# A chunked two-way RWKV-7 recurrence: the loop over chunks written out on four engines, and two small tiles read in place

## The chip, the cores and the metric

The kernel runs on 1 core of one Trainium2 chip. The metric is the device time of one execution in microseconds (us), smaller is better. The program computes a whole network of two blocks. The change touches one stage of it, the recurrence of the second block's RWKV mixer; all other stages are the same in both kernels.

## What is computed in the stage

The reference, cut to the recurrence (all float32). `x` has 512 latent tokens, the context has 256; there are 16 heads of 64. The recurrence runs forward and backward, first over the context and then, from the context's final states, over the latents.

```python
def _rwkv_step(S, inp):
    r, w, kk, kka, kt, v = inp
    sk = jnp.einsum('bhij,bhj->bhi', S, kk)
    S = S * w[:, :, None, :] - sk[..., None] * kka[:, :, None, :] + v[..., None] * kt[:, :, None, :]
    return S, jnp.einsum('bhij,bhj->bhi', S, r)

# in stream(h, S0): low-rank inputs of the decay and of the rate, one pair for each direction z
dec = w0[:, None, None, :] + jnp.einsum('zbtr,zrd->zbtd', jnp.tanh(jnp.einsum('btd,zdr->zbtr', xw, w1)), w2)
logw = -jax.nn.softplus(-dec) - 0.5
w = heads(jnp.exp(-jnp.exp(logw)))
a = heads(jax.nn.sigmoid(a0[:, None, None, :] + jnp.einsum(
    'zbtr,zrd->zbtd', jnp.einsum('btd,zdr->zbtr', xa, a1), a2)))
...
S_f, y_f = _rwkv_scan(S0[0], (r, w[0], kk, kk * a[0], kt[0], v), False)
S_b, y_b = _rwkv_scan(S0[1], (r, w[1], kk, kk * a[1], kt[1], v), True)
```

## The kernel before, in words

The four compute engines run programs of their own and meet at semaphores. `rwkv_scan` takes the tokens in chunks of 64 (`CH`), in two phases: the context (4 chunks, `lat` false) and the latents (8 chunks, `lat` true). Both directions z = 0 and z = 1 are walked alternately, so that one direction's work fills the other's waits. A call of `both(z, it, y, tail_it, front_it)` is one **step**, and it weaves three things together on every engine:

- the **chain** of direction z, chunk `it`: Gram matrices (`gram`), five levels of squaring of a 64x64 matrix per head (`level`), with the results copied out of PSUM by ScalarE and VectorE and the unit matrix added by GpSimd (`factor`);
- the **tail** of direction y, chunk `tail_it`: `start`, six products `apply` with a copy by ScalarE (`x_out`) between each two, `results`, and `state`, whose product VectorE adds to the state (L2644);
- the **front** of direction y, chunk `front_it`: `decay_rank` and `rate_rank` (TensorE, from the low-rank inputs, called latents), then gates, `cumulate`, keys, `alpha`, `beta`, `kappa`, `rho`, and `end` on GpSimd.

`in_turn` sets the order: two steps ahead of the loop, then a hardware loop (`eng.Fori`, L2188) over `steps - 1` iterations of two steps each, then two steps behind it. Each engine runs this loop itself, with its own counter and its own backward branch. In it a wait compares a semaphore with a value in a register, which register instructions work out from the counter, since the value grows with the iteration (`Events.value`). The loop has 3 iterations in the context phase and 7 in the latent phase, so TensorE's branch goes back 2 + 6 = 8 times.

On TensorE each wait goes through `wait` (L2318), which is an instruction of its own and also adds 1 to a semaphore `begun`, which nobody reads.

The low-rank inputs of all tokens stand in `tw` and `ta`, in the buffer X. GpSimd's `latents` (L2211) copies this step's 64 columns of each into the small tiles `twc` and `tac`; TensorE reads them in `decay_rank` (L2339) and `rate_rank` (L2347). `latents` comes first in a step on GpSimd, thus behind `decayed` and `end` of the step before. TensorE waits for "tokens" before `decay_rank`, and `gram` stands behind `decay_rank` in its queue.

In the program a float32 matmul stands once; in the trace it is two MATMUL with two LDWEIGHTS.

## Time and profile before

| | |
|---|---|
| time, median of 3 runs | 4123.04 us (4122.61 to 4123.76) |
| time of the profiled execution | 4099.76 us |
| its span | 4098.0 us |
| granted TensorE clock, mean of the span | 0.91 |
| the recurrence, from the first step with a chain to the last product | 2579 to 3375 us of the span |

The profile is of one execution, which took 23 us less than the median of the others. The recurrence holds about a fifth of the span. In the rows, PE is a matmul, PEld the load of its weights, PEldq, ACTq, DVEq and POOLq are the engines' sequencers (branches, register instructions and waits), and "idle before <-X" tells what ended the engine's idle time. "issue" is time in which the engine waited for nothing that the profile shows.

### The profile page before, as it was taken

The numbers are of one execution on the slowest core, as the hardware profiler recorded it, in microseconds if no ns is written. First come the engines' busy times: TensorE is split into PE (matmuls) and PEld (weight loads), VectorE is DVE, ScalarE is ACT, GpSimd is POOL, SyncE is SP. The second block draws the span as 40 slices with busy tenths as digits, with TensorE's granted clock in tenths as the row PEclk, the third lists the DMA queues.
The fourth block names the chain that finished last, engine by engine and source line by source line (L and its number), as shares of the span: only waits on it lengthen the run. The fifth ranks groups of instructions, "written<-read, shape, count | busy, mean of one in ns | idle before, by whom it ended". The sixth has DMA issues, their size and how long they took to land. (4 is left out here: it accounts for less than half of the span.)

```text
span 4098.0 us, 85586 instructions
## 1 busy us (share of the span) xinstructions
PE 3343.7 (82%) x37286; PEld 1973.3 (48%) x37286; DVE 1463.6 (36%) x3061; ACT 811.7 (20%) x1666; POOL 462.1 (11%) x448
## 2 busy tenths in 40 slices
PE   6998999896999986999995898776777765678877
PEld 5846476463445643343342444666666662322222
DVE  3656256552025623212213412443444434311111
ACT  2015111241015610000001001443333320100000
POOL 0000000000001100000000000443433320000000
PEclk9998899988999987999997998897989877799999
DMA  5652247302111124999996110000000002299998
GB/s 163 164 186 74 50 118 190 117 22 83 57 48 33 60 82 176 365 346 336 363 345 228 49 48 21 4 4 3 4 4 4 4 13 100 100 399 404 404 402 347
DMA packets 148963, 606.63 MB, mean 148 GB/s; under 512 B 19200, under 2 KB 21824, under 8 KB 131584
## 3 DMA queue, kind: packets, MB, share of 16 engines
q1 hardware_dynamic: 142272, 579.57, 39.0%
q0 software_dynamic: 6336, 21.63, 2.3%
q8 instruction: 308, 5.05, 0.5%
q14 instruction: 47, 0.39, 0.0%
HBM read 576.39 MB, written 31.07 MB: 148 GB/s over the span
## 5 line engine op out<-in xcount | busy, mean ns | idle before, releaser
L1704 PE MATMUL psum<-ring,big 128*64 128x512 f32 (+1 forms) x6144 | 904.8, 500 | 110.2 <-DMA ring<-moe_w 93.6
L1704 PEld LDWEIGHTS psum<-ring,big 128*64 128x64 f32 (+1 forms) x6144 | 301.4, 125 | 674.4 <-issue 472.6
L2297 PE MATMUL psum<-ring 64*64 64x64 f32 x11520 | 250.4, 232 | 100.8 <-issue 75.5
L371 PE MATMUL psum<-h_uT,ring 128*128 128x264 f32 x1280 | 290.5, 387 | 0.0
L2297 PEld LDWEIGHTS psum<-ring 64*64 64x64 f32 x11520 | 218.6, 143 | 129.2 <-issue 117.9
L371 PEld LDWEIGHTS psum<-h_uT,ring 128*128 128x128 f32 x1280 | 242.0, 190 | 46.5 <-issue 5.8
L500 DVE SCALAR_TENSOR_TENSOR h_O<-h_O,cond_silu 128x512 f32<-128x512 f32 x336 | 227.1, 743 | 102.2 <-DMA h_O<-ada_w 102.2
L1215 PE MATMUL psum<-ring,big 128*128 128x512 f32 x576 | 251.1, 596 | 2.0 <-PEq L55 2.0
L1985 PE MATMUL psum<-big,ring 128*128 128x512 f32 (+1 forms) x464 | 171.4, 532 | 31.7 <-DVE big L1956 24.0
L1850 DVE TENSOR_TENSOR big<-big,psum 128x512 f32<-128x512 f32 (+1 forms) x48 | 27.3, 596 | 463.7 <-PE psum L1704 463.7
L2234 POOL TENSOR_TENSOR ring<-ring,eye_sb 128x512 f32<-128x512 f32 x120 | 154.0, 1283 | 222.8 <-PE psum L2297 221.5
L1215 PEld LDWEIGHTS psum<-ring,big 128*128 128x128 f32 x576 | 109.0, 191 | 134.8 <-issue 134.8
L391 PE MATMUL psum<-ring,h_uT 128*128 128x512 f32 x384 | 168.3, 595 | 0.0
L2517 ACT ACTIVATE ring<-psum 128x512 f32<-128x512 f32 x168 | 100.4, 598 | 336.3 <-PE psum L2297 333.1
L1858 DVE SCALAR_TENSOR_TENSOR big<-psum,big,gates 64x512 f32<-64x512 f32 (+1 forms) x128 | 78.8, 615 | 242.8 <-PE psum L1704 241.4
L1001 PE MATMUL psum<-ring,big 128*128 128x512 f32 x320 | 141.3, 605 | 11.0 <-DMA ring<-rw_w_o 9.4
L1985 PEld LDWEIGHTS psum<-big,ring 128*128 128x128 f32 x464 | 90.0, 195 | 112.9 <-issue 108.8
L1784 ACT ACTIVATE big<-psum 128x512 f32<-128x512 f32 (+1 forms) x48 | 23.5, 524 | 566.8 <-PE psum L1704 566.7
L2651 DVE COPY ring<-psum 128x512 f32<-128x512 f32 x96 | 66.4, 691 | 173.7 <-PE psum L2297 173.7
L391 PEld LDWEIGHTS psum<-ring,h_uT 128*128 128x128 f32 x384 | 72.0, 190 | 90.2 <-issue 90.1
L119 PE MATMUL psum<-ident_sb,big 128*128 128x128 f32 x176 | 29.0, 343 | 97.0 <-DVE big L197 97.0
L1001 PEld LDWEIGHTS psum<-ring,big 128*128 128x128 f32 x320 | 61.9, 194 | 89.1 <-issue 79.6
(344 smaller groups left out, 4544.7 us busy)
## 6 DMA issues: line engine op xcount, KB each, us to landing
ring<-moe_w SPq DMA_DIRECT2D x192, 2048.0 KB, 10.8
h_O<-ada_w SPq DMA_DIRECT2D x192, 256.0 KB, 3.0
ring<-w_in SPq DMA_DIRECT2D x16, 2048.0 KB, 14.8
ring<-na_w_qkv SPq DMA_DIRECT2D x6, 2048.0 KB, 8.0
ring<-w_out SPq DMA_DIRECT2D x4, 2048.0 KB, 8.8
bias_rows<-na_table SPq DMA_DIRECT2D x16, 480.0 KB, 15.7
ring<-bias_rows SPq DMA_DIRECT2D x16, 360.0 KB, 2.9
rows<-big SPq DMA_DIRECT2D x10, 512.0 KB, 5.1
```

Source lines behind the costliest of these rows:

```text
L371: last = nc.tensor.matmul(bank(k, pair_bank(q) + h, NH), w[:, a, f * P:(f + 1) * P], uT[:, a, halves[h]], start=a == 0, stop=a == KD - 1)
L391: last = nc.tensor.matmul(bank(k, b), uT[:, a, t * P:(t + 1) * P], w[:, a, :], **st)
L500: nc.vector.scalar_tensor_tensor(into, ada(u), by, into, ALU.mult, ALU.add).then_inc(s.acc, 1)
L1001: last = nc.tensor.matmul(bank(k, j % BANKS)[0:rows, :], srcT[:, a, t * P:t * P + rows], w[:, a, :], start=a == 0, stop=a == KD - 1)
L1215: last = nc.tensor.matmul(bank(k, j % FIRST_BANKS), hT[:, a, t * P:(t + 1) * P], w[:, a, :], start=a == 0, stop=a == KD - 1)
L1704: last = nc.tensor.matmul(bank(k, b, r.width)[q * r.n:(q + 1) * r.n, :], rowsT[:, half * HALF_K + n, r.first:r.first + r.n], w[:, n, q * r ...
L1858: last = nc.vector.scalar_tensor_tensor(y[r.first:r.first + r.n, x % 2, cols], bank(k, r.downs, r.width)[mine, :], gate[mine, x, 2 * r.at ...
L1985: last = nc.tensor.matmul(bank(k, j % BANKS, n), w[:, a, at:at + P], xs[m][:, a, first:first + n], **st)
L2234: ev["pool"][z].done(nc.gpsimd.tensor_tensor(pairs(factors[n], z), pairs(factors[n], z), eye3, ALU.add), f"factor{n}")
L2297: last = nc.tensor.matmul(bank(k, b, CH, at + p % QUAD * CH)[to:to + CH, :], pairs(lhs, z)[lo:lo + CH, p, :], rhs(lo, p), start=start and ...
L2517: ev["act"][z].done(nc.scalar.activation(flat2(T_n, z), side(W(z), 0), ACT.Copy), f"x{n}")
L2651: ev["dve"][z].done(nc.vector.tensor_copy(both_of(n, z, 1), bank(k, U(z) + 1).rearrange("p (e x) -> p e x", e=2)), f"level{n}")
```

## The change

- `in_turn` runs a Python loop instead of `eng.Fori`. The steps of all iterations stand one behind another in the program, on TensorE, ScalarE, VectorE and GpSimd, in the same order as they were run. The values that waits compare with, and the columns that are read, are constants.
- GpSimd's `latents` is gone, with the tiles `twc` and `tac` and the events "tokens" and "rates". `decay_rank` and `rate_rank` read 64 columns of `tw` and `ta` directly, and do not wait for GpSimd.
- TensorE's `wait` no longer adds to `begun`. Where a wait stands just ahead of a matmul the builder now puts it on the matmul itself.

```diff
@@ -2122,7 +2122,7 @@
-        pool=["tokens", "rates", "akk"] + only("bon", "bonus_in") + ["end"])
+        pool=["akk"] + only("bon", "bonus_in") + ["end"])
@@ -2185,7 +2185,7 @@
             both(0, 0, 1, None, 0)
-            with eng.Fori(0, steps - 1) as it:
+            for it in range(steps - 1):
                 both(1, it, 0, it, it + 1)
                 both(0, it + 1, 1, it, it + 1)
@@ -2208,20 +2208,6 @@
-                def latents(z, it, tail_it):
-
-
-                    mine, lo = fr["pool"][z], z * CH
-                    if tail_it is not None:
-                        made("pe", z, tail_it, "iclr")
-                    elif lat:
-                        pool.wait_ge(fr["pe"][z].sem, fr["pe"][z].before(0))
-                    c = columns_of(it, z, steps, first)
-                    mine.done(nc.gpsimd.tensor_copy(twc[lo:lo + CH, :], tw[lo:lo + CH, bass.ds(c, CH)]), "tokens")
-                    made("pool", z, it, "tokens")
-                    mine.done(nc.gpsimd.tensor_copy(tac[lo:lo + CH, :], ta[lo:lo + CH, bass.ds(c, CH)]), "rates")
-                    made("pool", z, it, "rates")
-
@@ -2318,8 +2302,6 @@
                     pe.wait_ge(sem, value)
 
-                    pe.sem_inc(s.begun, 1)
-
@@ -2333,18 +2315,16 @@
-                    lo = z * CH
-                    made("pool", z, it, "tokens")
+                    lo, at = z * CH, columns_of(it, z, steps, first)
                     for half in range(2):
-                        last = nc.tensor.matmul(bank(k, U(z))[half * CH:(half + 1) * CH, :], twc[lo:lo + CH, :],
+                        last = nc.tensor.matmul(bank(k, U(z))[half * CH:(half + 1) * CH, :], tw[lo:lo + CH, at:at + CH],
                                                 w2[lo:lo + CH, half * BANK:(half + 1) * BANK], start=True, stop=True)
                     fr["pe"][z].done(last, "dec")
 
                 def rate_rank(z, it):
-                    lo = z * CH
-                    made("pool", z, it, "rates")
+                    lo, at = z * CH, columns_of(it, z, steps, first)
                     for p in range(PAIRS):
-                        last = nc.tensor.matmul(bank(k, U(z) + 1, CH, p * CH), a2[lo:lo + CH, p * P:(p + 1) * P], tac[lo:lo + CH, :],
+                        last = nc.tensor.matmul(bank(k, U(z) + 1, CH, p * CH), a2[lo:lo + CH, p * P:(p + 1) * P], ta[lo:lo + CH, at:at + CH],
                                                 start=True, stop=True)
```

What stands in TensorE's queue, before, at the end of the context phase's loop: the last products of `state`, then the counter and the branch back.

```order
L2297 MATMUL psum<-ring,X 64x64 x4
L2297 MATMUL psum<-X,ring 64x64 x4
L2188 REGISTER_ALU
L2188 COMPARE_AND_BRANCH
L2297 MATMUL psum<-X,big 64x64 x2
```

The last row is the code behind the loop; the branch goes back over the whole body, 804 matmuls of the program in this phase and 996 in the other. The same place now, on TensorE, with the next step's `start` (X,big and X) directly behind `state`:

```order
L2281 MATMUL psum<-ring,X 64x64 x4
L2281 MATMUL psum<-X,ring 64x64 x4
L2281 MATMUL psum<-X,big 64x64 x2
L2281 MATMUL psum<-X 64x64 x2
L2281 MATMUL psum<-X,big 64x64 x2
```

The counter and the branch have gone, and nothing has come between the two steps. Register instructions between the products of a step are gone too. TensorE before, in the loop's first step, from the end of `start` over `decay_rank`, `gram` (on big) and `rate_rank` to the first level (ISA is a pair of register instructions in one):

```order
L2297 MATMUL psum<-X 64x64 x2
L2319 REGISTER_ALU
L2319 ISA
L2339 MATMUL psum<-ring,rw_twc 64x512 x2
L2319 REGISTER_ALU
L2297 MATMUL psum<-big 64x64 x32
L2319 REGISTER_ALU
L2347 MATMUL psum<-rw_tac,ring 128x64 x8
L2319 ISA
L2319 REGISTER_ALU x2
L2297 MATMUL psum<-ring 64x64 x16
```

Each of these places holds the value that the next wait compares with. And now, the same step, where `decay_rank` and `rate_rank` read X:

```order
L2281 MATMUL psum<-X 64x64 x2
L2320 MATMUL psum<-ring,X 64x512 x2
L2281 MATMUL psum<-big 64x64 x32
L2327 MATMUL psum<-X,ring 128x64 x8
L2281 MATMUL psum<-ring 64x64 x64
```

The products and their order are the same; only what stood between them is gone.

## Rows read from the trace of the kernel before

**Rows 1.** The page, its first line.

```profile
span 4098.0 us, 85586 instructions
```

**Rows 2.** By stretch: us, busy of PE, PEld, DVE, ACT, POOL, PEclk, DMA share, GB/s.

```profile
2579.20:2799.00 219.80, 160.93 (x6394) 143.76 (x6392) 94.06 (x128) 96.65 (x153) 81.98 (x81) 0.91 0.02 4
2799.00:3375.00 576.00, 414.88 (x15948) 374.43 (x15940) 242.74 (x368) 202.91 (x319) 215.39 (x208) 0.86 0.02 4
...
2899.40:2935.60 36.20, 26.37 (x1000) 23.50 (x1002) 15.38 (x23) 12.76 (x20) 13.11 (x13) 0.86 0.02 5
2935.60:2967.10 31.50, 22.75 (x996) 20.51 (x996) 15.02 (x24) 12.70 (x20) 13.68 (x13) 1.00 0.02 4
```

**Rows 3.** Waits in 2579:3375: who <- whom, us in total, times, longest.

```profile
ACT ring L2517 <- PE psum L2297: 333.1, 103, 13.6
...
PEld psum L2297 <- issue: 217.3, 241, 4.4
...
PE psum L2297 <- issue: 102.0, 98, 2.1
...
PE psum L2339 <- POOL rw_twc L2220: 21.2, 12, 5.5
```

**Rows 4.** Groups by line, 2579:3375: the products of start, idle before them.

```profile
L2297 PE MATMUL psum<-X,big 64*64 64x64 f32 x768 | 42.4, 264 | 40.3 <-POOL rw_tac L2222 19.6 <-POOL rw_twc L2220 10.7 <-issue 8.7
```

**Rows 5.** Line 2188, the branch: duration ns min/median/max, first and last start.

```profile
L2188 PEldq COMPARE_BRANCH  x10: 83/3356/3858, 2647.7 to 3321.5; - x10
...
L2188 POOLq COMPARE_BRANCH  x10: 44/50/58, 2650.7 to 3324.8; - x10
```

**Rows 6.** Timeline of PE behind one branch back: start, us, [idle before].

```profile
2971.29 0.51 PE L2297 MATMUL psum<-X,big 64*64 64x64 f32 x8 [4.29 <-POOL rw_tac L2222]
...
2973.43 0.26 PE L2297 MATMUL psum<-X,big 64*64 64x64 f32 x1 [1.06 <-issue]
```

**Rows 7.** Timeline of DVE: the state's addition, which ends each step.

```profile
2648.17 0.69 DVE L2644 TENSOR_TENSOR X<-X,psum 128x512 f32<-128x512 f32 x1 [1.85 <-PE psum L2297]
...
2677.37 0.69 DVE L2644 TENSOR_TENSOR X<-X,psum 128x512 f32<-128x512 f32 x1 [1.70 <-PE psum L2297]
...
2702.66 0.69 DVE L2644 TENSOR_TENSOR X<-X,psum 128x512 f32<-128x512 f32 x1 [1.29 <-PE psum L2297]
...
2899.45 0.69 DVE L2644 TENSOR_TENSOR X<-X,psum 128x512 f32<-128x512 f32 x1 [0.84 <-PE psum L2297]
...
2935.61 0.69 DVE L2644 TENSOR_TENSOR X<-X,psum 128x512 f32<-128x512 f32 x1
...
2967.07 0.69 DVE L2644 TENSOR_TENSOR X<-X,psum 128x512 f32<-128x512 f32 x1 [0.24 <-PE psum L2297]
```

**Rows 8.** Timeline of PE from one issue gap to the next, inside a step.

```profile
2957.19 1.35 PE L2297 MATMUL psum<-ring 64*64 64x64 f32 x73 [1.51 <-issue]
2958.33 0.68 PE L2297 MATMUL psum<-gates 64*64 64x64 f32 x32
2958.80 0.49 PE L2441 MATMUL psum<-head_ones_sb,ring 64*64 64x1 f32 x21
2960.71 0.39 PE L2441 MATMUL psum<-head_ones_sb,ring 64*64 64x1 f32 x11 [1.42 <-issue]
```

**Rows 9.** DMA queues in 2579:3375: packets, MB, share of 16 engines.

```profile
q8 instruction: 193, 3.16, 1.6%
q14 instruction: 5, 0.04, 0.0%
```

**Rows 10.** Lines 2319 and 2321, TensorE's register instructions and waits: count, ns.

```profile
L2319 PEldq ALU_OP  x381: 32/32/38, 2595.6 to 3314.1; - x191
...
L2321 PEldq EVENT_SEMAPHORE  x868: 51/51/51, 2567.3 to 3369.1; - x174
```

**Rows 11.** Timeline of PE: decay_rank at the latents' second step, and in a step.

```profile
2815.70 1.12 PE L2339 MATMUL psum<-ring,rw_twc 64*64 64x512 f32 x2 [5.52 <-POOL rw_twc L2220]
...
2939.29 0.65 PE L2339 MATMUL psum<-ring,rw_twc 64*64 64x512 f32 x2 [0.95 <-POOL rw_twc L2220]
```

More of the change, by code:

```diff
@@ L2137, in rwkv_scan @@
     w2, a2, w0 = (lora2[:, n * D:(n + 1) * D] for n in range(3))
-    twc, tac, d_end = small
+    d_end = small
     own = lambda t, z: t[:, z * BANK:(z + 1) * BANK]
@@ L2168, in rwkv_scan @@
     names = " ".join(f"{n}{z} {n}_front{z}" for n in engines for z in range(DIRS))
-    with stage(k, "cleared begun " + names) as (block, s):
+    with stage(k, "cleared " + names) as (block, s):
         def phase_list():
@@ L2265, in both @@
                     chain, front, tail = z is not None, front_it is not None, tail_it is not None
-                    if front:
-                        latents(y, front_it, tail_it)
                     if chain:
@@ L2812, in rwkv_layer @@
         R = sb("R", [P, KD, SEQ])
-        twc, tac = sb("twc", [P, CH]), sb("tac", [P, CH])
         d_end = sb("d_end", [P, DIRS * PAIRS])
@@ L2831, in rwkv_layer @@
         room += [held[:, n * D:(n + 1) * D] for n in range(4)] + [apart[:, n * D:(n + 1) * D] for n in range(5, 8)]
-        rwkv_scan(k, K, KK, R, V, tw, ta, Y, bonus, slot(0), room, apart, (twc, tac, d_end))
+        rwkv_scan(k, K, KK, R, V, tw, ta, Y, bonus, slot(0), room, apart, d_end)
         mixT = flat(C)[:, 0:KD * SEQ].rearrange("p (a b) -> p a b", a=KD)
```

## The prediction, made before the changed kernel was run

> **What bounds the kernel now.** I read the stretches first. The recurrence takes 219.8 us in the context phase and 576.0 us in the latent phase [rows 2] of a span of 4098.0 [rows 1]. Nothing outside it is changed, so everything is decided there. TensorE is the busiest engine in both stretches (160.93 and 414.88 us), the others are busy less than half of the time, so I read next who waits for whom. ScalarE's copies between the products wait 333.1 us for TensorE, and TensorE itself waits mostly for nothing that the profile shows: 217.3 us in 241 places ahead of a weight load, 102.0 us in 98 places ahead of a matmul [rows 3]. The chain of waits that ended last is of little use here, since it reaches back only through the expert layers behind this stage.
>
> What "issue" is can be seen in a timeline. Between two such gaps there stand 73 + 32 + 21 = 126 matmuls, with as many weight loads, and the next gap comes after TensorE has been at work for some 2 us; the gaps are 1.51 and 1.42 us [rows 8]. The queue that fetches instructions moved 193 packets in the recurrence, 3.16 MB, thus 16 KB each [rows 9]. The matmuls of both phases are 22,342 and the loads as many [rows 2], with 868 waits and 381 register instructions on their lines [rows 10]; with the loop's own and the fused ones, 46,105 instructions (counted in the built program with the loops multiplied out). If a packet is 256 of them, 193 packets are 49,408, and two gaps 256 apart fit the 126 pairs of rows 8. So I read it thus: TensorE fetches its instructions in blocks of 256, the next block isn't asked for early enough, and the 796 us from 2579 to 3375 go by at 796/193 = 4.1 us a block. The loop keeps nothing: its body of some 4,100 instructions is fetched anew each time.
>
> **The branch back.** TensorE's branch takes 3356 ns in the median, and 83 ns where it falls through (twice of ten); GpSimd's takes 50 ns [rows 5]. Behind one of them TensorE stands for 4.29 us, works a little, and stands again for 1.06 us, since the loop's head lies inside a block and the next block has only then been asked for [rows 6]. The profile puts these waits down to GpSimd's copies, which happened to end nearby: 19.6 + 10.7 us in 8 places ahead of `start` [rows 4], and there are 8 branches back. `start` doesn't wait for the copies at all; a theory built on that label would give GpSimd the blame. The cost of the branch is best read from step to step. From state to state, a step that begins with a branch back takes 2935.61 - 2899.45 = 36.2 us, the next one, with the same work for the other direction and no branch, 2967.07 - 2935.61 = 31.5 us [rows 7]. Over the six such pairs of the latent phase the means are 37.8 and 32.7, a difference of 5.0; in the context phase 2677.37 - 2648.17 = 29.2 against 2702.66 - 2677.37 = 25.3 [rows 7], 3.9, and the same once more. Written out, all steps are of the second kind: 6 x 5.0 + 2 x 3.9 = **38 us**. Its lower bound is the branch alone, 8 x 3.36 = 27 us. In the difference of 5.0 the clock has a part: granted 0.86 in the step with the branch, 1.00 in the other [rows 2]; that is 2.4 GHz throughout in the one, and some 1.2 GHz after the stall in the other.
>
> The Trainium skill (Advanced Engine Details and Errata, Control Flow Timing) gives about 108 ns for a compare-and-branch. By that figure this term would be an estimate of under 1 us instead of 38; the 83 ns that falls through and GpSimd's 50 ns agree with it, the 3356 ns of TensorE's doesn't, so the row decides.
>
> **Fewer instructions on TensorE.** Counted in the built program: before, 869 waits, 488 register instructions, the loops' 12; now 321 waits of their own, while 453 stand on a matmul. 1,048 of 46,105 instructions go, that is 4.1 blocks. Upper bound at the mean of 4.1 us a block: 17 us. Lower bound 0, if those blocks are the ones in which TensorE waits for data anyway. Between these I go by the gaps: 98 matmuls waited for issue alone, for 1.0 us in the mean [rows 3], which is over half of 193 blocks, and 1.4 of the 3.5 us from 2957.19 to 2960.71 stand open [rows 8], so most blocks are bound by the fetch. I take **15 us**. The same count checks the first term: 193 fetched and 180 executed leave 13 blocks that were fetched and thrown away around 8 branches, and 13 + 4 = 17 blocks fewer at 4.1 would be 70 us, against the 53 of the two terms together; the thrown-away ones are partly hidden.
>
> A second rule of the Trainium skill bears on this term: Runtime: NRT & Kernel Launch, Instruction fetch mechanics, says that crossing a block of 16 KiB is mostly hidden, as the next is fetched during the current one. By it these 15 us would be 0. The gaps of 1.51 and 1.42 us speak against it here; it makes the first rival.
>
> **Latents in place.** Two copies of 0.23 us by GpSimd go from each step; GpSimd is the least busy but one in the latent phase (215 of 576 us [rows 2]), and its own time costs nothing. What counts is TensorE's wait for the first of them, 21.2 us in 12 places [rows 3]. It falls in two kinds. At the head of the latent phase it is 5.52 us in one place [rows 11]; there `decay_rank` stood behind GpSimd's work for the other direction. Without it, `gram` is late next, for it needs VectorE's `kappa` of the first front; of the 5.5 us I take 2. A like wait at the end of the context phase and two short ones at the stage's first fronts add some 2.5. Within the steps it is 0.95 us at a time [rows 11], about ten times. In a block that is paced by the fetch, such a wait only shortens the gap at its end, so I count 3 of these 10 us. Together **7 us**, between 0 and 21. Reading X instead of a small tile changes neither a shape nor a partition of the operands: 64 rows by 64 columns of float32 both ways, at nothing.
>
> **The other engines' code.** In the loop, ScalarE, VectorE and GpSimd ran out of what they had fetched: 5 packets of 8 KB on their queue in all [rows 9]. Written out they have 480, 565 and 483 instructions, in all some 12 such packets. I cost this at nothing, since a packet lasts these engines for two to three steps (60 us or more), many times what a fetch takes. If that cover failed, each would cost up to a branch's 3.4 us, some 40 us in all; that is the third rival.
>
> **The sum.** 38 + 15 + 7 = 60 us. The profiled execution was 4099.8 us with a span of 4098.0, so a profiled execution of the changed kernel should have a span near 4038. The median of the runs was 4123.0; the loss is in the same instructions there, so I take the 60 off it: **4063 us**, 1.5% less. About 0.2% or 8 us is what a measurement of this kernel can tell from no change.
>
> **The rivals.**
> First, crossings hidden, only the branch counts. The instructions that go are worth nothing, and the gaps in rows 8 are something else, such as a queue that fills. Then the gain is 38 + 5 = 43 us: 4080. For it: a weight load's wait for issue is 0.9 us in the mean [rows 3], so many are shorter than those of rows 8. Against it: their spacing of 126 pairs.
> Second, the seam is bound by the chain through the others. When TensorE's branch ends, VectorE has added the state and GpSimd has scaled it. If the next step needed these, only about 1 us of each stall would be won, 8 in all, and 6 to 10 for the rest: 4107. Against it: `start` of the other direction needs nothing that was made after the previous step, and the steps without a branch show what the seam costs otherwise.
> Third, slower: code that is no longer resident stalls ScalarE, VectorE or GpSimd in the chain. Each of 12 crossings then holds up the step as TensorE's branch does, and by what the branch costs (5.0), that is 60 us, which takes the whole gain back. From over 5 us a crossing the kernel is slower; with 8 us each, as when the fetch queues behind TensorE's that is always under way, it would be 4063 + 96 = 4159. Against it: on the page's other stages these engines fetch straight code all the time, and their waits for issue are not among the costly ones.
> Fourth, better than forecast: steps go at the pace of the shortest blocks. With 7.8 blocks of 3.5 us, as the one in rows 8, a step of the latent phase takes 27 instead of 32.7 us. If a quarter of that is reached over 20 steps, 25 us come on top: 4038.
>
> **Chances.** The forecast 0.62, the first rival 0.15, the second 0.05, the third 0.05 (a little of it near no change), the fourth 0.13. The forecast's own bounds are from 4123 - 83 = 4040 (17 and 21 us for the last two terms, with some of the rest) to 4123 - 30 = 4093 (branch alone). The range 4036 to 4092 takes in the first rival and most of the fourth. Faster by over 0.2%: 0.92; within: 0.03; slower: 0.05.
>
> **What would show it.** No branch between steps on TensorE, and the steps of the latent phase all near 32 us from state to state, without the alternation of 37.8 and 32.7. The fetch queue at 176 packets (45,057 instructions) instead of 193 in the recurrence, at 4.1 us each; the gaps of 1 to 1.5 us still there every 126 to 128 matmuls. The other queue at about 17 packets instead of 5, with no idle time of ScalarE, VectorE or GpSimd that ends on issue. The recurrence from the first chain to the last product near 796 - 58 = 738 us. If the packets fall to 176 and the time falls by less than 45 us, the second term is wrong; if steps that open a packet on one of the other engines are longer than their neighbours, the third rival is at work; and if the time outside the recurrence moves by over 5 us, something that I have not seen.

## The result, and the profile after

The changed kernel takes 3990.93 us in the median of 4 runs (3989.15 to 3996.73), against 4123.4 us before (4122.61 to 4123.99). The ratio is 0.9681, with an interval of 0.9665 to 0.9698: 132 us less, 125 to 138. I had forecast 60 us less (4063, range 4036 to 4092). The sign was right; the size was less than half of what came, and the time lies outside the range. Ratios and intervals here leave out the one execution of all that fell far out of line, of 11,034 us, among ten of the kernel in which only the other engines' loops are written out; what held it up is not known.

The page of the changed kernel, its first line and the busy time of the engines, which answer to [rows 1]:

```profile
span 3994.9 us, 83561 instructions
...
PE 3286.3 (82%) x37286; PEld 1928.5 (48%) x37286; DVE 1462.5 (37%) x3061; ACT 803.6 (20%) x1666; POOL 451.9 (11%) x400
```

The span is 103 us shorter than that of rows 1. The two profiled executions thus show 103 of the 132 us; that of before was 23 us below its median, that of after 6 us above. The 23 us go with the clock. Over 45 other executions of the kernel before, which took 4109.6 to 4147.5 us, TensorE's mean granted clock was 0.896 to 0.907, on the whole the lower the longer; a straight line through them (an estimate from these runs) gives 29 us for each 0.01, and 4103 us at 0.910, the clock of the profiled execution, which took 4099.76.

Where the 103 us went is told by stretches, first of before, then of after (us; busy of PE, PEld, DVE, ACT, POOL; granted clock; DMA share; GB/s). The first one ends ahead of the stage. The second is the recurrence, from its first product to its last.

```profile
0.00:2560.00 2560.00, 2242.65 (x12533) 1243.39 (x12534) 962.13 (x2282) 463.08 (x1125) 100.96 (x112) 0.93 0.44 149
2567.00:3374.00 807.00, 584.50 (x22368) 524.14 (x22368) 341.08 (x501) 304.96 (x479) 300.62 (x295) 0.87 0.02 4
```

```profile
0.00:2560.00 2560.00, 2239.99 (x12534) 1242.66 (x12534) 961.89 (x2282) 462.93 (x1125) 100.79 (x112) 0.93 0.44 149
2567.00:3271.00 704.00, 528.11 (x22368) 479.46 (x22368) 340.40 (x502) 297.00 (x479) 290.28 (x247) 0.91 0.02 4
```

The recurrence went from 807 to 704 us, which is the whole difference; ahead of it nothing moved, and behind it 724 us are left in both. The 22,368 matmuls are the same, but TensorE is busy with them for 56 us less, at a granted clock of 0.91 instead of 0.87; the other 47 of the 103 us are idle time. VectorE and ScalarE do the same work; GpSimd has 48 instructions fewer, the copies.

The additions to the state, which answer to the first three of [rows 7] (timeline of VectorE: start, us, ..., [idle before]), and two of the latent phase:

```profile
2642.23 0.69 DVE L2624 TENSOR_TENSOR X<-X,psum 128x512 f32<-128x512 f32 x1 [0.45 <-PE psum L2281]
2666.46 0.69 DVE L2624 TENSOR_TENSOR X<-X,psum 128x512 f32<-128x512 f32 x1 [1.82 <-PE psum L2281]
2690.40 0.69 DVE L2624 TENSOR_TENSOR X<-X,psum 128x512 f32<-128x512 f32 x1 [0.83 <-PE psum L2281]
...
2900.59 0.69 DVE L2624 TENSOR_TENSOR X<-X,psum 128x512 f32<-128x512 f32 x1 [0.57 <-PE psum L2281]
2929.46 0.69 DVE L2624 TENSOR_TENSOR X<-X,psum 128x512 f32<-128x512 f32 x1 [0.24 <-PE psum L2281]
2958.27 0.69 DVE L2624 TENSOR_TENSOR X<-X,psum 128x512 f32<-128x512 f32 x1 [0.24 <-PE psum L2281]
```

Two steps of the context that took 29.2 and 25.3 us take 24.2 and 23.9. In the latent phase the steps are 28.9 and 28.8 us here; over the six pairs the means were 37.8 and 32.7 and are now 29.5 and 29.2. So the alternation is gone, as forecast. (28.8 is a step that began with a branch before.) But the steps without a branch, whose length I took as the new one for all, became 3.5 us shorter themselves. That is the first sign that the error isn't in the branch.

The waits in the stretch of the stage, which answer to [rows 3] (who <- whom: us in total, times, longest):

```profile
ACT ring L2497 <- PE psum L2281: 268.3, 99, 7.6
...
PEld psum L2281 <- issue: 144.5, 144, 2.1
...
PE psum L2281 <- issue: 124.5, 111, 2.0
```

TensorE still waits mostly for nothing that the profile shows. The matmuls' waits for issue are as many as before, 124.5 us in 111 places on this line and 4.9 in 3 on `head_ones`' line, against 102.0 in 98 and 18.8 in 14; the weight loads' waits fell from 217.3 to 144.5 us and from 241 places to 144. The queues that fetch instructions, in the recurrence:

```profile
q8 instruction: 177, 2.90, 1.8%
...
q14 instruction: 11, 0.09, 0.0%
```

Over the same boundaries the kernel before has 194 and 5. The forecast was 176 instead of 193, and about 17 on the other queue. The gaps of [rows 8] are still there (timeline of TensorE, start, us, ..., [idle before]):

```profile
2942.18 0.92 PE L2281 MATMUL psum<-ring 64*64 64x64 f32 x44 [1.54 <-issue]
2943.02 1.16 PE L2338 MATMUL psum<-running_sb,ring 64*128 64x128 f32 x16
2944.11 1.26 PE L2281 MATMUL psum<-ring 64*64 64x64 f32 x66
2946.09 0.63 PE L2281 MATMUL psum<-ring 64*64 64x64 f32 x27 [0.72 <-issue]
```

44 + 16 + 66 = 126 matmuls again, 252 instructions with their loads, and the rest are waits. The blocks are thus what I took them for, their number is as forecast, and their price is 704/177 = 3.98 us instead of 807/194 = 4.16. 17 blocks fewer at 4.16 us are 71 us, and 177 blocks that are 0.18 us shorter are 32 us: together the 103 us of the two spans. What made the blocks shorter, and which part of the change took which share, is for the experiments.

### The profile page after: what moved, and what is told of

It reads as the page before. It is cut to its first block and busy times, and to the rows that moved or that the text cites. A ratio compares the mean times of both kernels' runs of the same rounds, so it can differ in the third digit from the quotient of the medians.

```text
span 3994.9 us, 83561 instructions
## 1 busy us (share of the span) xinstructions
PE 3286.3 (82%) x37286; PEld 1928.5 (48%) x37286; DVE 1462.5 (37%) x3061; ACT 803.6 (20%) x1666; POOL 451.9 (11%) x400
## 5 line engine op out<-in xcount | busy, mean ns | idle before, releaser
L2281 PE MATMUL psum<-ring 64*64 64x64 f32 x11520 | 227.1, 226 | 91.2 <-issue 73.4
L2281 PEld LDWEIGHTS psum<-ring 64*64 64x64 f32 x11520 | 202.2, 140 | 105.2 <-issue 79.8
L1215 PEld LDWEIGHTS psum<-ring,big 128*128 128x128 f32 x576 | 108.4, 190 | 133.7 <-issue 133.7
L1784 ACT ACTIVATE big<-psum 128x512 f32<-128x512 f32 (+1 forms) x48 | 23.5, 524 | 564.8 <-PE psum L1704 564.7
L119 PE MATMUL psum<-ident_sb,big 128*128 128x128 f32 x176 | 29.5, 348 | 97.1 <-DVE big L197 97.1
L1790 ACT ACTIVATE big<-psum 128x512 f32<-128x512 f32 (+1 forms) x48 | 25.2, 526 | 397.9 <-PE psum L1727 397.9
```

The source lines that it names most:

```text
L1215: last = nc.tensor.matmul(bank(k, j % FIRST_BANKS), hT[:, a, t * P:(t + 1) * P], w[:, a, :], start=a == 0, stop=a == KD - 1)
L2281: last = nc.tensor.matmul(bank(k, b, CH, at + p % QUAD * CH)[to:to + CH, :], pairs(lhs, z)[lo:lo + CH, p, :], rhs(lo, p), start=start and ...
```

## The experiments

Each kernel was measured in one session with the kernel before. The ratio is that of the medians, in brackets its interval. The recurrence runs from its first product to its last, in the profiled execution of each; "clock" is TensorE's granted clock in it, and "blocks" the packets of TensorE's fetch queue, to within one. "Lone waits" are the instructions on TensorE's queue that only wait; the others sit on a matmul.

| kernel | us | ratio | recurrence, us | clock | blocks | lone waits |
|---|---|---|---|---|---|---|
| before | 4123.4 | 1 | 807 | 0.87 | 194 | 869 |
| the changed kernel | 3990.93 | 0.9681 [0.9665, 0.9698] | 704 | 0.91 | 177 | 321 |
| the same, second time | 3991.45 | 0.9679 [0.9659, 0.9700] | 709 | 0.90 | 175 | 321 |
| the same, third time | 3994.51 | 0.9680 [0.9655, 0.9705] | 700 | 0.91 | 177 | 321 |
| TensorE's loop alone written out | 4081.95 | 0.9868 [0.9840, 0.9897] | 790 | 0.86 | 178 | 869 |
| the other engines' alone | 4129.29 | 0.9985 [0.9968, 1.0003] | 834 | 0.85 | 194 | 869 |
| all written out | 4079.26 | 0.9860 [0.9832, 0.9888] | 793 | 0.86 | 178 | 869 |
| and no `begun` | 4037.26 | 0.9765 [0.9736, 0.9794] | 734 | 0.90 | 176 | 341 |
| the changed kernel with `begun` | 4043.74 | 0.9817 [0.9797, 0.9837] | 747 | 0.88 | 178 | 821 |
| each wait twice | 4024.11 | 0.9762 [0.9741, 0.9782] | 735 | 0.89 | 179 | 821 |
| each wait twice, with `begun` | 4046.09 | 0.9798 [0.9777, 0.9819] | 756 | 0.87 | 178 | 821 |
| fewest waits | 3994.93 | 0.9699 [0.9671, 0.9728] | 702 | 0.90 | 176 | 191 |
| copies back, unread | 3996.02 | 0.9683 [0.9658, 0.9708] | 704 | 0.91 | 175 | 321 |
| 12 blocks more | 4038.33 | 0.9790 [0.9766, 0.9814] | 739 | 0.92 | 187 | 321 |
| two wide products a chain | 4002.47 | 0.9702 [0.9677, 0.9727] | 712 | 0.91 | 176 | 321 |
| two products in one | 3983.93 | 0.9657 [0.9635, 0.9678] | 691 | 0.92 | 172 | 321 |
| the same again | 3985.98 | 0.9660 [0.9634, 0.9685] | 687 | 0.90 | 172 | 321 |

### The loop, engine by engine

First the loop on TensorE alone. The copies, `begun` and the other engines' loops stay. (`two` holds the loop's body, two steps.)

```diff
+            if eng is pe_eng:
+                for it in range(steps - 1):
+                    two(it)
+            else:
+                with eng.Fori(0, steps - 1) as it:
+                    two(it)
```

> The kernel before with TensorE's loop alone written out; ScalarE, VectorE and GpSimd keep theirs, the copies of the latents and the semaphore begun stay. Theory A (the gain is TensorE's branch and its fewer instructions): 38 us for the branch plus 500 register instructions or 2 blocks at 4.1 us, 46 us below before: 4077. Theory B (the register instructions of the other engines delay each of their waits, some 3 us a step): 4077 as well, since theirs stay. Theory C (what the prediction missed is on TensorE, in the register instruction and the two separate waits between a copy's end and the next product): 4050 or less.

The ratio is 0.9868: 54 us less, 42 to 66. Three additions to the state in the latent phase, where the middle one ends a step that began with a branch before:

```profile
2970.50 0.69 DVE L2652 TENSOR_TENSOR X<-X,psum 128x512 f32<-128x512 f32 x1 [0.84 <-PE psum L2305]
3004.08 0.69 DVE L2652 TENSOR_TENSOR X<-X,psum 128x512 f32<-128x512 f32 x1
3036.70 0.69 DVE L2652 TENSOR_TENSOR X<-X,psum 128x512 f32<-128x512 f32 x1 [1.01 <-PE psum L2305]
```

33.6 and 32.6 us. Over the six pairs the means are 34.1 and 32.7, from 37.8 and 32.7 before. The second kind of step is as long as it was in the profile of before, so the rule "all steps as the ones without a branch" holds for this edit, but for 1.4 us a pair that stay in the first kind. That the two figures agree so closely owes something to which execution was profiled: in the trace of the next kernel, where TensorE's loop stands as before and the granted clock was 0.85, the means of the two kinds are 39.8 and 33.1 us. The 1.4 us have a name in the waits of this kernel, the small tile that GpSimd copies:

```profile
PE psum L2347 <- POOL rw_twc L2228: 44.3, 22, 6.8
```

Before, over the same stretch from the first product on, it was 28.0 us in 13 places ([rows 3] begins later, with 12 of them):

```profile
PE psum L2339 <- POOL rw_twc L2220: 28.0, 13, 6.8
```

The branch's stall had hidden this wait at the seams; with the branch gone it stands at nearly every `decay_rank`.

The opposite edit, ScalarE, VectorE and GpSimd written out and TensorE's loop kept:

```diff
+            if eng is not pe_eng:
+                for it in range(steps - 1):
+                    two(it)
+            else:
+                with eng.Fori(0, steps - 1) as it:
+                    two(it)
```

> The kernel before with the loops of ScalarE, VectorE and GpSimd written out and TensorE's kept. Theory A: no change, 4123 within 5. Theory B: 30 to 60 us less, 4065 to 4095, with steps some 2 us shorter. If code that is not resident stalls these engines, slower than 4130.

0.9985, with 1 inside the interval. The other queue, in the recurrence of this kernel:

```profile
q14 instruction: 12, 0.10, 0.0%
```

12 packets instead of 5, and no cost of them to be seen. (The 834 us in the table are of a profiled execution of 4132 us, 33 more than that of before, at a granted clock of 0.85 in the stage instead of 0.87; the ratio is of the medians.) The third rival falls, and these engines' register instructions were worth no more than the interval allows, 13 us. Both together, with `begun` and the copies still there:

> All four loops written out, copies and begun kept: this part of the change alone. Theory A: 4077, the same as with TensorE alone. Theory B: 4020 to 4045. If the parts add up, the sum of the gains of the two runs above.

0.986: 58 us less, 46 to 69. TensorE's part, 54 us, is all of it within the intervals.

### The increments and the waits

From the last kernel the line that adds to `begun` is taken out, and the builder then puts waits on matmuls where it can.

```diff
                     pe.wait_ge(sem, value)
 
-                    pe.sem_inc(s.begun, 1)
-
```

> All loops written out and begun gone, so that 478 waits stand on matmuls and 341 alone (869 alone with begun); the copies of the latents stay. Theory A (instructions cost only their fetch): 528 instructions or 2.1 blocks, 8 us less than with begun. Theory C (each wait of its own, with an increment, costs time in the chain product, copy, product): over 20 us less than with begun, and what then separates it from the changed kernel (3991) is the latents' part, forecast as 7 us.

0.9765 against 0.986: 39 us. My forecast had priced this part at 2 blocks, about 8 us. The blocks did fall by 2 only (178 to 176), so the 39 us are something else. The reverse, from the changed kernel, with the changed kernel itself measured again beside it:

```diff
                     pe.wait_ge(sem, value)
 
+                    pe.sem_inc(s.begun, 1)
+
```

> The changed kernel once more, beside the three that follow. 0.968 of before, as first measured, near 3995.

> The changed kernel with begun back: loops written out, latents read in place, 821 waits alone on TensorE instead of 321. Theory A (528 to 500 instructions cost their fetch alone): 8 us more than the changed kernel. Theory C (a wait alone costs some 0.08 us wherever it stands, as between the two runs with the copies, 42 us for 528): 40 us more, near 4035. If in-place reading and begun overlap, less than 30 more.

The changed kernel gave 3991.45 us (0.9679) again, and 4043.74 with `begun`: 52 us for a line whose result nobody reads. It does two things: it adds an increment to each wait, and it keeps 453 waits from being carried by a matmul. To part them, each wait is issued twice, without an increment. The first of the two is then alone and the second can be carried:

```diff
                 def wait(sem, value):
                     pe.wait_ge(sem, value)
+                    pe.wait_ge(sem, value)
```

> The changed kernel with every wait of TensorE in the recurrence issued twice: 821 waits alone, 453 on matmuls, no increment; the second one of each pair is met at once. If what costs is an instruction of its own on TensorE's sequencer (Theory C), the same as with begun, 35 to 45 us more than the changed kernel. If it is the increment or the loss of the wait on the matmul, clearly less than with begun, 10 us more or below. Theory A: 2 blocks, 8 us more.

4024.11 us against 3991.45 beside it: 33 us for 500 lone waits more, all of them either already met or the first of a pair; 66 ns each. The source view of one of the two lines shows what the trace itself gives each of them (duration min/median/max in ns):

```profile
L2304 PEldq EVENT_SEMAPHORE  x500: 51/51/1463, 2575.5 to 3299.3; - x167
```

500 x 51 ns = 25 us of the 33. Then the same with an increment on each of the 820 lone ones:

```diff
                 def wait(sem, value):
                     pe.wait_ge(sem, value)
+                    pe.sem_inc(s.begun, 1)
                     pe.wait_ge(sem, value)
```

> The changed kernel with every wait of TensorE in the recurrence issued twice and begun raised by the first: 820 waits alone with an increment, 453 on matmuls. The doubled waits without increments cost 33 us against the changed kernel, begun as before (821 alone, one on a matmul) 52. If the increments make the difference, 0.981 of before, as with begun. If it is that no wait stands on a matmul, 0.976, as with the doubled waits.

0.9798 against 0.9762: 15 us more for 820 increments, some 18 ns each. The two were measured in different sessions and the difference is uncertain by 12 us, so that an increment costs something is barely shown, and its size is rough. The ratio is also near the 0.9817 of the kernel with `begun` alone, although here 453 waits sit on matmuls again. So no gain from being carried by a matmul could be measured beyond that of not being an instruction by itself. The weight loads' idle time for issue is longer too, in the kernel with `begun` and in that with each wait twice, against 144.5 us in 144 places of the changed kernel:

```profile
PEld psum L2281 <- issue: 202.3, 194, 4.6
```

```profile
PEld psum L2281 <- issue: 151.7, 139, 2.4
```

In the first it is 58 us longer, as much as the extra 52 us, in the second 7 us longer, a fifth of its 33. The part of a doubled wait that isn't seen as idle time of the loads is open.

If a lone wait costs 66 ns, 130 fewer should give 9 us. Waits that an earlier one implies are left out here:

```diff
+            seen = {}
             for lat, steps, first, chunk, ev, fr in phase_list():
                 def wait(sem, value):
+                    if seen.get(sem.name, 0) >= value:
+                        return
+                    seen[sem.name] = value
                     pe.wait_ge(sem, value)
...
-                    after("pool", z, it, "values")
+                    after("pool", z, it, f"factor{LAST - 1}")
```

The last two lines are in `start`, which now waits once for GpSimd's last factor, so that later waits on GpSimd are implied by it.

> The changed kernel without the waits on TensorE that an earlier wait on the same semaphore covers, and with one wait of start for GpSimd's last factor instead of five later ones: 191 waits alone instead of 321, 429 on matmuls instead of 453. Theory C: 130 x 0.08 = 10 us less than the changed kernel. Theory A: 0.6 blocks, 2 us less, that is no difference.

3994.93 against 3991.45: no gain in the medians. The profiled recurrence is shorter (702 against 709 us for the changed kernel measured beside it), so a gain of a few us isn't excluded, but it isn't shown either. By the two ratios, 0.9699 and 0.9679, some 6 us is the most that could have been gained. The 66 ns are thus a price for waits added everywhere, and not shown for each one taken away.

### The latents

The kernel without `begun` but with the copies, against the changed one, gives the latents' part: 0.9765 to 0.9679, 35 us (with `begun` kept in both, 0.9860 to 0.9817, 18 us). Is it TensorE's wait or GpSimd's time? The copies are put back into the changed kernel, where nothing reads them:

```diff
+                    mine.done(nc.gpsimd.tensor_copy(twc[lo:lo + CH, :], tw[lo:lo + CH, bass.ds(c, CH)]), "tokens")
...
+                    mine.done(nc.gpsimd.tensor_copy(tac[lo:lo + CH, :], ta[lo:lo + CH, bass.ds(c, CH)]), "rates")
...
                 def both(z, it, y, tail_it, front_it):
                     chain, front, tail = z is not None, front_it is not None, tail_it is not None
+                    if front:
+                        latents(y, front_it)
```

> The changed kernel with GpSimd's copies of the latents back in their old place in its queue, but TensorE reads in place and waits for none of them. If the latents' part is TensorE's wait (40 to 45 us idle ahead of decay_rank in 22 places once the loops are written out), this is as fast as the changed kernel, within 5 us. If it is GpSimd's time or its later work, 15 to 35 us more.

0.9683, as the changed kernel. GpSimd's time for the copies is free, and TensorE's wait is left as the cause. (The copies' own wait, for TensorE's `rate_rank` of the step before, was not put back, so what it may have cost GpSimd is in neither kernel.) The waits' view of the kernel written out without `begun`, in which the copies are still read:

```profile
PE psum L2343 <- POOL rw_twc L2226: 45.0, 23, 6.8
```

Without the first of them, 6.8 us, it is 38.2 us in 22 places, and 35 us were gained. The first stays in another name: the source view of `decay_rank` in the changed kernel has, as what ended its idle time,

```profile
  issue: 9.0, 5
  POOL rw_bonus L2198: 6.4, 1
  DVE ring L2620: 2.8, 2
```

where line 2198 clears a tile at the stage's start, which the first product has to wait for in either kernel.

Why did these waits cost nearly their full length? TensorE's instructions can be counted in the traces, 256 by 256 from the stage's start, which gives the blocks themselves. In the kernel with the copies the blocks that hold a `decay_rank` take 5.44 us in the median, in the changed kernel 4.46; all other blocks take 3.73 in both. And those blocks of the changed kernel end with a gap of only 0.20 us in the mean, while the others end with one of 1.05. There was hardly a gap at their end that a wait could have been hidden in.

### Is a block of instructions what paces TensorE?

If it is, instructions cost and array time doesn't. Two kernels set the one against the other; both have extra products whose results are overwritten. One forms the two products of `rows` twice, which adds 128 instructions on TensorE to each of the 24 chains, 12 blocks in all:

```diff
                     heads(W(z), 0, z, (T_beta, eye))
+                    heads(W(z), SIDE, z, (T_kappa, eye))
+                    heads(W(z), 0, z, (T_beta, eye))
                     ev["pe"][z].done(heads(W(z), SIDE, z, (T_kappa, eye)), "rows")
```

> The changed kernel with the products of rows made twice into the same place: 32 matmuls of the program more in each of 24 chains, that is 128 instructions or half a block, 12 blocks in all, of 64 columns each. Theory F (TensorE's pace is its fetch, 4.0 us a block): 48 us more. If it is bound by what waits for data, up to 28 us (24 times 1.2 us of matmuls), less where there is slack.

The other adds two products of 512 columns a chain, with 8 instructions:

```diff
+                    for n in range(2):
+                        nc.tensor.matmul(bank(k, W(z))[0:CH, :], tw[0:CH, 0:CH], w2[0:CH, 0:BANK], start=True, stop=True)
```

> The changed kernel with two more products of 64x512 in the same 24 places, whose results are overwritten: 8 instructions each time, 0.75 of a block in all, but some 0.9 to 1.7 us of the array. Theory F: 3 to 10 us more, since the gap at the block's end takes the rest. If the array's time counts in full, 21 to 40 us more.

The recurrence in the two, first the kernel with 12 blocks more, by stretch and then by its fetch queue, and below it that with the wide products:

```profile
2570.00:3310.00 740.00, 551.50 (x23904) 502.24 (x23904) 338.89 (x501) 297.48 (x479) 292.26 (x249) 0.92 0.02 4
```

```profile
q8 instruction: 187, 3.06, 1.7%
```

```profile
2568.00:3280.00 712.00, 569.49 (x22464) 494.80 (x22464) 337.91 (x501) 296.02 (x479) 291.56 (x247) 0.91 0.02 4
```

```profile
q8 instruction: 176, 2.88, 1.7%
```

Against the changed kernel's 528.11 us, TensorE is busy for 23 us more in the first and for 41 us more in the second. The time moves the other way round: against the kernel with unread copies, which was measured beside them and is as fast as the changed one, the first is 42 us slower and the second 6.5. What counts is the number of instructions, 42/12 = 3.5 us a block (the intervals leave 14 us on the 42), and the array has room of its own. That the instructions cost by their fetch, and not one by one, isn't told by these two kernels but by where the gaps stand.

That shows in the trace of the changed kernel, by counting TensorE's instructions from the first one of the recurrence: 104 of the some 110 places where it goes on after waiting for issue fall on one and the same count modulo 256. With the two kernels it settles the first rival, crossings hidden, against it. Where TensorE goes on from such a place, the next packet never starts earlier than 1.04 us after (median 1.21), and TensorE goes on again some 2.5 us after that packet's start (median). Packets follow each other at 3.27 us at the least and 3.77 us in the median, and the 3.5 us that each of the 12 added blocks cost lie between. With `begun` the median of the first part is 1.45 us, and 1.62 before; without `begun` but with the copies it is 1.23. This fits blocks that got shorter as their first instructions ran more quickly, and with them the request for the next; no experiment isolates it.

### A kernel with fewer instructions

If blocks count, products can be merged. In the latent phase `kappa` is multiplied with `alpha` and with `rho`, head by head, with the same operand loaded. With `alpha` and `rho` side by side in a tile it is one matmul of 2 x 64 columns, and `raised_r` takes what is left. 1,024 instructions go, 4 blocks; the work is the same.

```diff
-                    last = heads(W(z), 0, z, (T_kappa, of(T_alpha, z)))
-                    if lat:
-                        last = heads(W(z), SIDE, z, (T_beta, of(T_rho, z)))
+                    if not lat:
+                        last = heads(W(z), 0, z, (T_kappa, of(T_alpha, z)))
+                    else:
+                        two = alpha_rho.rearrange("p (e x) -> p e x", e=2)
...
+                                    last = nc.tensor.matmul(into, pairs(T_kappa, z)[lo:lo + CH, p, :], two[lo:lo + CH, :, at:at + CH],
+                                                            start=True, stop=True)
...
-                    heads(W(z), 0, z, (T_kappa, of(T_rho, z)))
+                    heads(W(z), 0, z, (T_beta, of(T_rho, z)))
```

> The changed kernel, the same result: in the latent phase the products of kappa with alpha and with rho, which have the same stationary operand, are one matmul with 2x64 moving columns (alpha and rho side by side in memory), and beta with rho takes the place of the second. 16 matmuls of the program fewer in each of 16 chains, 1024 instructions or 4 blocks, with the same columns in the array. Theory F (the fetch sets the pace, 4.0 us a block): 16 us less than the changed kernel, 0.964 of before. If the array's columns or the waits for data set it: no difference, 0.968.

3983.93 us, 0.9657, the fastest kernel of the study. As the changed kernel hadn't been measured beside it, both were run once more, side by side:

> The changed kernel beside the one with two products in one, on the same chip, since the last comparison of the two (0.9679 and 0.9657 of before, in different calls) doesn't part them.

> The same kernel as e14, beside the changed kernel. Theory F: 16 us less than it. If the pace is set otherwise: no difference. The runs in different calls stood 9 us apart.

3985.98 against 3994.51 us: 8.5 us less, where 4 blocks at 4 us had let me expect 16. The ratios (0.9660 and 0.9680) have intervals that overlap, so neither the size nor, strictly, the sign is settled; both measurements of this kernel lie below all three of the changed one. The recurrence by stretch, and its fetch queue:

```profile
2567.00:3259.00 692.00, 523.69 (x21856) 476.20 (x21856) 340.79 (x501) 297.55 (x479) 292.76 (x249) 0.92 0.02 4
```

```profile
q8 instruction: 172, 2.82, 1.8%
```

## Why the prediction was right in its sign and short in its size

The parts of the change as the runs measured them, against the terms of the sum. The register instructions and the waits were one term there; here they are split by their share of its 4.1 blocks.

| part | forecast | measured | from |
|---|---|---|---|
| branch and register instructions of TensorE | 38 + 7 | 58 (46 to 69) | all written out |
| `begun`, with the waits that matmuls now carry | 8 | 39 | the same without `begun` |
| latents in place | 7 | 35 | from there to the changed kernel |
| the other engines' code | 0 | 0 (interval: 13 less to 1 more) | the others' loops alone |
| sum | 60 | 132 | |

The 39 and the 35 are differences of two ratios, uncertain by 14 to 17 us each. They also depend on their order: with `begun` kept, the latents are worth 18 us, and `begun` is worth 52 once they are in place. The sum doesn't depend on it.

**What bounds the kernel** was read rightly. Blocks of 256 instructions pace TensorE, 12 more cost 42 us, and the number of packets came to 177, where 176 was forecast. The Trainium skill (Runtime: NRT & Kernel Launch, Instruction fetch mechanics) says that a crossing is mostly hidden. The runs disagree: a block that is added costs 3.5 us here.

**The branch back** was right in its mechanism and, within the interval, in its size. TensorE's loop alone gave 54 us (42 to 66) where 38 + 7 were forecast, the alternation from step to step is gone, and the profile's label on those stalls, GpSimd's copies, was rightly not believed at the seams. The second rival (only 1 us a seam won) falls with it. Left out was that the same copies then become a real wait: 13 places before, 22 with the branch gone.

**Fewer instructions on TensorE** is the first step that failed: 8 of its 15 us were for the waits, and these measured 39. I priced a wait by its 1/256 of a block, 16 ns, and the register instructions likewise. The view of [rows 10] had their durations in plain sight, 51 ns for each of 868 waits and 32 ns for a register instruction, and I used only their counts. With `begun` back in the changed kernel, and nothing else, the weight loads were idle for issue 58 us longer. From rows 10, 548 fewer waits at 51 ns would have been 28 us and 381 register instructions at 32 ns another 12, so 40 us where I took 15. Doubled waits measured 66 ns each, and the increment on top perhaps 18 ns, of which I had thought not at all. I had set the upper bound of this term at 17 us, by blocks alone; a bound has to be drawn by each way in which an instruction can cost, and the queue's own time was one.

**Latents in place** is the second. The mechanism, TensorE's wait and not GpSimd's time, was right. The rule that a wait inside a block "only shortens the gap at its end", by which I counted 3 us of 10, was wrong, and so was the number of places. 38.2 us stood in 22 places once the branch and `begun` were gone, and 35 came back: nearly all of it. The rule needs a gap at the block's end, and the blocks that hold `decay_rank` have one of only 0.20 us. Only the head of the latent phase went as said. `gram` is late next there, and waits 2.8 us for VectorE:

```profile
PE psum L2281 <- DVE gates L2591: 2.8, 1, 2.8
```

That is TensorE's longest wait in 2790 to 2840 of the changed kernel; before, 9.1 us in three places stood in this stretch, 5.52 of them as in [rows 11].

**The other engines' code** was rightly costed at nothing; 11 packets came instead of some 17.

**The fourth rival**, steps at the pace of the shortest blocks, was nearest, and had a chance of 0.13. But it was told as a matter of the fetch alone, while the runs put the rest in the two terms above, and its 25 us more would have left it at 4038, still 47 us short. That all rivals but one lay on the side of a smaller gain came from the same place: each term of the sum had its upper bound from the same mechanism.

**The clock** is the rival that the runs leave open. The whole executions of the changed kernel had a mean granted clock of 0.914 to 0.921, those of before 0.896 to 0.907, and among those of before a higher clock went with a shorter time. So a part of each gain may have come by way of the clock and not directly by the edit; which leads, no run tells. It doesn't set the time by itself: the kernel with 12 blocks more had the highest clock in the recurrence, 0.92, and was 42 us slower, and the kernel with two products in one took 691 us there at 0.92 and 687 at 0.90. My step from the profile to the median, the same 60 us off both, took no account of it either. Why 130 fewer waits gave nothing is open too.

## What to carry to other kernels

Where the engine with small products waits for "issue", count its instructions by kind and price each twice, by its share of a fetched block and by its own duration on the queue; take the larger as the upper bound. A semaphore increment or a wait that nobody needs wasn't free here, though the engine is shown as idle beside it. Before a wait is priced low because a gap follows it, look whether its own block has such a gap. When a large stall goes, list the waits that it had covered before costing the next edit at its old price, and treat edits whose gains overlap as one sum.

## What the runs showed of the hardware

- TensorE's fetch: blocks of 256 instructions, packets at least 3.27 us apart in the changed kernel, 3.98 us a block in its mean and 4.16 before; 12 blocks more cost 42 us, while 41 us more of array work cost 6.5 us.
- A lone wait takes 51 ns on TensorE's queue when nothing holds it, and 500 more of them cost 33 us; 130 fewer gave nothing that could be measured. A wait that a matmul carries had no price that could be measured.
- An increment on a lone wait cost some 18 ns (820 for 15 us, uncertain by 12).
- Blocks that hold a `decay_rank` took 5.44 us in the median with its wait for GpSimd and 4.46 without; all others took 3.73 in both.
- Written out, ScalarE, VectorE and GpSimd fetched 12 packets instead of 5 in the stage, and no loss could be measured (the interval allows 1 us).
